# A two-layer hybrid block: the first two output slabs worked by halves, and three steps moved between engines

## What is computed

```python
def mixer_ab(u, pos, w_in, w_out, ...):
    z = u @ w_in
    za, zb = z[..., :A_IN], z[..., A_IN:]
    ...
    ya = diff_attention(qa, ka, va, lam, subln_g, lambda_init)
    yb = rwkv7_time_mix(zb, mu, w0, w2, a0, a2, g2, k_k, k_a, r_k, lnx_g, lnx_b)
    return jnp.concatenate([ya.astype(u.dtype), yb.astype(u.dtype)], axis=-1) @ w_out
```

```python
    y = wkv7_scan(heads(r), heads(decay), heads(k), heads(v), -kk, kk * heads(a).astype(jnp.float32))
    mu_y = jnp.mean(y, axis=-1, keepdims=True)
    var_y = jnp.mean(jnp.square(y - mu_y), axis=-1, keepdims=True)
    y = (y - mu_y) * lax.rsqrt(var_y + LNX_EPS)
    y = y * lnx_g... + lnx_b...
    bonus = jnp.sum(heads(r) * heads(k) * r_k, axis=-1, keepdims=True) * heads(v)
    y = (y + bonus.astype(jnp.float32)).reshape(B, T, B_WIDTH) * g.astype(jnp.float32)
```

## Time and profile before

| what | value |
|---|---|
| median of three runs | 2696.46 us (2686.87 to 2701.3) |
| the profiled execution, its own time | 2687.12 us |
| its span, first to last instruction | 2685.4 us |
| TensorE busy | 2525.0 us, 94% of the span |
| VectorE, ScalarE, GpSimd busy | 1443.8, 1082.8 and 266.1 us |
| mean granted TensorE clock | 0.976 of full speed |

### The profile page before, as it was taken

One profiled execution on the slowest core, in us unless ns is written; L12 is line 12 of the kernel. 1 busy time (PEld: TensorE's weight loads), 2 busy tenths in 40 slices (PEclk: granted clock), 3 DMA queues, 4 the chain that ended last, 5 costly groups with the idle time before them and its releaser, 6 DMA issues.

```text
span 2685.4 us, 33969 instructions
## 1 busy us (share of the span) xinstructions
PE 2525.0 (94%) x14359; PEld 2083.3 (78%) x14359; DVE 1443.8 (54%) x1447; ACT 1082.8 (40%) x1167; POOL 266.1 (10%) x239
## 2 busy tenths in 40 slices
PE   8999987889999999999988998898999999999897
PEld 6887767678888878878766977786888888888775
DVE  4566774645544445445454567646544545445454
ACT  4455420344434334334434444545434334334432
POOL 3001343111000000000122000012000000000121
PEclk9999999999999999999998999998999999999998
DMA  7556401356555555555543654255555565555542
GB/s 260 187 176 206 137 26 68 133 180 207 184 192 188 188 175 186 190 178 181 188 142 103 192 176 152 75 192 192 188 188 189 187 195 187 188 196 179 181 144 75
DMA packets 224819, 453.22 MB, mean 169 GB/s; under 512 B 7833, under 2 KB 16343, under 8 KB 223403
## 3 DMA queue, kind: packets, MB, share of 16 engines
q1 hardware_dynamic: 218816, 430.11, 48.5%
q0 software_dynamic: 3648, 17.54, 1.9%
q10 hardware_dynamic: 2219, 3.59, 0.5%
HBM read 445.52 MB, written 2.10 MB: 167 GB/s over the span
## 4 chain that ended last, share of the span: by engine, by line
PE 85%; DVE 8%; ACT 3%; issue 2%; ACTq 1%; DMA 0%; SPq 0%; DVEq 0%
PE psum L294 26%; PE psum L296 26%; PE psum L295 26%; DVE wlo L276 2%; ACT whi L272 2%; DVE h L441 1%; PE psum L596 1%; PE psum L712 1%; PE psum L318 1%; PE psum L1444 1%; PE psum L1440 1%; PE psum L1425 0%; ACT junk L386 0%; ACTq L992 0%; DVE m L686 0%
## 5 line engine op out<-in xcount | busy, mean ns | idle before, releaser
L276 DVE TENSOR_TENSOR wlo<-raw,whi 128x2048 fp32r<-128x2048 f32 (+1 forms) x404 | 929.9, 2302 | 1057.0 <-ACT whi L272 1056.8
L272 ACT ACTIVATE whi<-raw 128x2048 fp32r<-128x2048 f32 (+1 forms) x408 | 775.0, 1900 | 1232.9 <-PE psum L296 1226.5
L294 PE MATMUL psum<-whi,uTh 128*128 128x512 f32 (+2 forms) x2240 | 882.7, 394 | 18.0 <-DVE uTl L340 10.7
L296 PE MATMUL psum<-whi,uTl 128*128 128x512 f32 (+2 forms) x2240 | 871.1, 389 | 6.3 <-issue 6.3
L295 PE MATMUL psum<-wlo,uTh 128*128 128x512 f32 (+2 forms) x2240 | 870.5, 389 | 0.0
L294 PEld LDWEIGHTS psum<-whi,uTh 128*128 128x128 f32 x2240 | 424.4, 189 | 111.2 <-issue 11.9
L296 PEld LDWEIGHTS psum<-whi,uTl 128*128 128x128 f32 x2240 | 423.7, 189 | 92.1 <-issue 7.2
L295 PEld LDWEIGHTS psum<-wlo,uTh 128*128 128x128 f32 x2240 | 424.2, 189 | 82.7 <-issue 1.7
L294 PE MATMUL psum<-whi,hTh 128*128 128x512 f32 x1024 | 400.6, 391 | 6.1 <-DVE wlo L276 6.1
L296 PE MATMUL psum<-whi,hTl 128*128 128x512 f32 x1024 | 398.6, 389 | 0.0
L295 PE MATMUL psum<-wlo,hTh 128*128 128x512 f32 x1024 | 398.5, 389 | 0.0
(11 more groups left out here) (348 smaller groups left out, 1493.8 us busy)
## 6 DMA issues: line engine op xcount, KB each, us to landing
raw<-in_w_mlp_up SPq DMA_DIRECT2D x128, 1024.0 KB, 5.2
raw<-in_w_mlp_down SPq DMA_DIRECT2D x128, 1024.0 KB, 5.1
raw<-in_ab_w_in SPq DMA_DIRECT2D x48, 1024.0 KB, 5.1
raw<-in_w_ple_gate SPq DMA_DIRECT2D x32, 1024.0 KB, 5.1
raw<-in_c_w_in SPq DMA_DIRECT2D x24, 1024.0 KB, 5.3
raw<-in_ab_w_out SPq DMA_DIRECT2D x16, 1024.0 KB, 5.3
raw<-in_c_w_out SPq DMA_DIRECT2D x16, 1024.0 KB, 5.0
raw<-in_c_w_in SPq DMA_DIRECT2D x12, 736.0 KB, 4.4
```

Source lines behind the costliest of these rows:

```text
L272: act.activation(whi[:, q % 2, :, 0:n], raw[:, q, :, 0:n], ACT.Copy).then_inc(hi_ready, 1)
L276: dve.tensor_tensor(wlo[:, q % 2, :, 0:n], raw[:, q, :, 0:n], whi[:, q % 2, :, 0:n].bitcast(F32), ALU.subtract).then_inc(lo_ready, 1)
L294: pe.matmul(o, xh, hi, start=(q == 0 and k == 0), stop=False)
L296: last = pe.matmul(o, xl, hi, start=False, stop=(q == 3 and k == 3))
```

## The change

Five things change, all within layer 0's mixer.

1. **Attention norm first.** `subln_dve` is cut in two. Its sum over squares (`subln_sum_dve`) moves ahead of `level_d_dve(0, 3)`, and its chain of tiny instructions (`subln_rms_dve`) goes to the place of the bonus sum. The bonus sum goes to the place of the old norm.
2. **Squares on ScalarE.** The squares of `out_norm_dve` part 2 become one ScalarE instruction for each token tile (`y_square_act`), between VectorE's centring and its sum.
3. **All lows on VectorE.** GpSimd no longer makes the lows of chunks 2 and 3 of the first output slab. VectorE's lows of chunks 0 and 1 are made earlier.
4. **Slabs in pairs.** The first two slabs of `ab_out` are worked as eight chunks: attention rows of slab 0, attention rows of slab 1, recurrence rows of slab 0, recurrence rows of slab 1. Loads, splits, matmuls and read-outs follow this order, and part 4 of `out_norm_dve` is cut into two parts (4 and 5), one for each half of the columns.
5. **Semaphores.** Two parameter loads now share one semaphore, and one step of `tt_init_pool` shares that of its setup.

```diff
-        dve.wait_ge(sem("bonus"), 2)
-        dve.tensor_reduce(bon[:], heads4(rkr[:]), AX.X, ALU.add).then_inc(sem("bon"), 1)
+        subln_rms_dve(dve, link)
         level_y_dve(dve, 0, 4)
         level_d_dve(dve, 1, 1)
         level_d_dve(dve, 0, 4)
-        subln_dve(dve, link)
+        dve.wait_ge(sem("bonus"), 2)
+        dve.tensor_reduce(bon[:], heads4(rkr[:]), AX.X, ALU.add).then_inc(sem("bon"), 1)
...
         u_out_dve(dve, 2)
+        split_lo(dve, base["ab_out"], 0)
         st_dve(dve, 2)
-        for k in range(4):
-            out_norm_dve(dve, link, 0, k)
-        prologue(split_lo, dve, "ab_out")
-        out_norm_dve(dve, link, 0, 4)
+        out_norm_dve(dve, link, 0, 0)
+        out_norm_dve(dve, link, 0, 1)
+        split_lo(dve, base["ab_out"], 1)
+        out_norm_dve(dve, link, 0, 2)
+        out_norm_dve(dve, link, 0, 3)
...
-        split_hi(act, base["ab_out"], 0)
+        prologue(split_hi, act, "ab_out")
         x_out_act(act, 3)
+        y_square_act(act, 0)
         u_out_act(act, 3)
-        split_hi(act, base["ab_out"], 1)
         y_out_act(act, 1)
+
+    def y_square_act(act, tt):
+        act.wait_ge(sem("y_centred"), tt + 1)
+        act.activation((sq0, Xs)[tt][:], rv[:, tt, :], ACT.Square).then_inc(sem("y_sq"), 1)
...
-        pool.wait_ge(lo_ready, 4 * base["ab_out"] + 2)
-        for q in (2, 3):
-            split_lo(pool, base["ab_out"], q)
...
+    OUT_CHUNKS = (((0, 0), (0, 1), (1, 0), (1, 1)), ((0, 2), (0, 3), (1, 2), (1, 3)))
...
+    def out_pair_pe(pe, st, src, ready):
+
+        T_pe(pe, st, src, ready, 0)
+        for v in range(2):
+            for q in range(4):
+                j, kc = OUT_CHUNKS[v][q]
+                s = base[st] + j
+                if v == 0 and q == 0:
+                    T_pe(pe, st, src, ready, 1)
+                if v == 0 and q == 2:
+
+                    pe.wait_ge(sem("y_out"), 2)
+                if v == 0 and q == 3:
+                    T_pe(pe, st, src, ready, 2)
+                    T_pe(pe, st, src, ready, 3)
+                pe.wait_ge(*mark("xT_lo", st, 2 * kc + 2))
+                pe.wait_ge(lo_ready, 4 * (base[st] + v) + q + 1)
...
-        pool.dma_start(p_ka[:], A["rwkv_k_a"][0].partition_broadcast(P)).then_inc(sem("ka_in"), 16)
+        pool.dma_start(p_ka[:], A["rwkv_k_a"][0].partition_broadcast(P)).then_inc(sem("ka_rk_in"), 16)
```

More of the change, by code:

```diff
@@ L747, in ple_dve, with out_keep_act @@
             step(split_lo, dve, s, st, W if j < 3 else next_width(st), gated, skip=(j == 0), last=(j == 3))
+    OUT_CHUNKS = (((0, 0), (0, 1), (1, 0), (1, 1)), ((0, 2), (0, 3), (1, 2), (1, 3)))
+    def out_keep_act(act, st, j, done):
+        s = base[st] + j
+        act.wait_ge(mm_used, done)
+        if j == 0:
+            act.wait_ge(*mark("xT", st, 8))
+        for tt in range(TT):
+            square(act, bank[2 * (s % 2) + tt][:], ssq[:, tt, j:j + 1], *mark("m_sq", st, 2 * j + tt + 1))
+        for tt in range(TT):
+            last = act.activation(m[:, tt, j * W:(j + 1) * W], bank[2 * (s % 2) + tt][:], ACT.Copy)
+        last.then_inc(sem("m_out"), 1)
@@ L750, in out_act @@
     def out_act(act, st):
+        s = base[st]
         if st == "ab_out":
             act.wait_ge(sem("y_mm"), 2)
[L754 to L768, removed]
@@ L770, in out_dve @@
-    def out_dve(dve, link, st):
[L771 to L778, removed]
-        if st == "ab_out":
-            dve.wait_ge(lo_ready, 4 * base[st] + 4)
-        for j in range(4):
-            step(split_lo, dve, base[st] + j, st, W if j < 3 else next_width(st), None, skip=(j == 0), last=(j == 3))
+            T_act(act, st, 0)
@@ new lines, in out_pair_pe @@
+    def out_pair_pe(pe, st, src, ready):
+        T_pe(pe, st, src, ready, 0)
+        for v in range(2):
+            for q in range(4):
+                j, kc = OUT_CHUNKS[v][q]
+                s = base[st] + j
+                if v == 0 and q == 0:
[7 more added lines that the diff above has]
+                pe.wait_ge(lo_ready, 4 * (base[st] + v) + q + 1)
+                for k in range(4):
+                    for tt in range(TT):
+                        o = bank[2 * (s % 2) + tt][:]
+                        xh = uTh[:, 4 * kc + k, tt * P:(tt + 1) * P]
+                        xl = uTl[:, 4 * kc + k, tt * P:(tt + 1) * P]
+                        hi, lo = whi[:, q % 2, k, :], wlo[:, q % 2, k, :]
+                        pe.matmul(o, xh, hi, start=(kc == 0 and k == 0), stop=False)
+                        pe.matmul(o, xh, lo, start=False, stop=False)
+                        last = pe.matmul(o, xl, hi, start=False, stop=(kc == 3 and k == 3))
+                last.then_inc(mm_used, 1)
@@ L785, in out_pe @@
     def out_pe(pe, st, src, ready):
-        for j in range(4):
-            if st == "ab_out" and j == 1:
-                pe.wait_ge(sem("y_out"), 2)
+        if st == "ab_out":
+            out_pair_pe(pe, st, src, ready)
+        for j in range(2 if st == "ab_out" else 0, 4):
             s = base[st] + j
```

92 lines of the change are left out of this document (71 added, 21 removed).

## The result

| what | before | after |
|---|---|---|
| median of six runs | 2693.86 us (2686.87 to 2702.59) | 2676.86 us (2671.26 to 2678.17) |
| profiled execution, and its span | 2687.12, 2685.4 | 2678.17, 2676.4 |
| mean granted TensorE clock | 0.976 | 0.975 |

The ratio is 0.9928, with a 95% interval of 0.9912 to 0.9943: 0.7% faster, 17.0 us by the medians. The forecast was 2677.9 us, a gain of 18.6. The profiled executions lie only 9.0 us apart. That of before lies at the low end of its runs, and that of after was the slowest of its six.

What follows compares the result with a forecast made beforehand. TensorE, busy 94% of the span, was taken as the bound, so only its waits could give time back. 11.7 + 8.1 - 1.2 = 18.6 us off the 2696.5 us median gave 2677.9 us, range 2664 to 2691.

Steps and rivals of the forecast that it cites:

- Term 1: Layer 0's mixer: with the attention norm moved, TensorE's wait for Y goes and the next link runs faster; 11.7 us gained.
- Term 2: End of the recurrence and first output chunks: TensorE starts earlier and the stage ends at 586.5 instead of 594.6; 8.1 us.
- Term 3: New TensorE pauses ahead of chunk 0 and chunk 2: lower clock after the latter loses 1.2 us, bounds 0 and 2.4.
- Copies beside GpSimd at 0: VectorE's PSUM copies of Xs and Us beside GpSimd's steps are not held: cost 0, bounded by 9.5 us.
- No slack for the squares: ScalarE's first squares end at 486.1, its last Us started at 486.09: each microsecond VectorE is late costs one.
- Only the norm pays: Rival, chance 0.15: VectorE bounds the first output chunks, whose gain falls to about 2 us; time 2684.
- Copies are held: Rival, chance 0.07: VectorE's copies of Xs and Us are held beside GpSimd, costing 9.5 us; time 2687.4.
- GpSimd holds the chain: Rival, chance 0.04: after the bonus sum GpSimd's steps hold thirteen VectorE chain instructions, costing 30.8 us; time 2708.7.
- the change does not do what it says: Rival, chance 0.04: the norm's tiny instructions stay slow in their new place, some 12 us; 2690 results.
- the sum is made on the profile and shifted to the median: Whole kernel: the 18.6 us worked out on the 2687.1 us profiled execution was subtracted unchanged from the 2696.5 us median.
- the sign that the prediction named against its chain as the path: Layer 0's mixer: if TensorE's 10.3 us pause goes but time falls under 10 us, the chain-is-the-path argument is wrong.

Runs made afterwards that it cites:

- x_late_again: Changed kernel with the reload of x issued behind the third slab's loads, measured once more as a base: 2669.21 us, ratio 0.9912.
- changed_again: The changed kernel itself, unaltered, measured once more: 2675.16 us, ratio 0.9942 to the kernel before.
- squares_dve: As x_late, with the squares of the output norm back on VectorE: 2667.8 us, ratio 0.9907.
- x_late: Changed kernel with the reload of x issued behind the third slab's loads instead of behind the first four chunks: 2668.3 us, ratio 0.9923.
- norm_undone: Changed kernel with the attention norm put back behind the bonus sum, all else as changed: 2681.65 us, ratio 0.9968.
- pool_quiet: Kernel before, with GpSimd waiting for the end of the attention norm before its eight bonus steps: 2685.67 us, ratio 0.9992.
- norm_only: Kernel before with only the attention norm moved ahead of the bonus sum: 2683.97 us, ratio 0.9976.
- x_shifted: Changed kernel with the reload of x held until the last state update is done: 2666.52 us, ratio 0.9918.
- lows_pool: As x_late, with the lows of the third and fourth chunk back on GpSimd: 2672.4 us, ratio 0.9924.

## Why the prediction was right, point by point

- **Term 1, 11.7 us.** Right in the trace. From the start of the chain's 128 matmuls to that of the next link it is 10.24 us less (forecast 10.25), and the link takes 2.08 us instead of 3.50, 1.42 less (forecast 1.45). The sum over squares in its new place cost nothing. SP's first load went out at 439.95 (forecast 438.7), and nobody waited for it. In the times of whole runs the norm's move brought 6.5 us, see below.
- **Term 2, 8.1 us.** Its mechanism was right and its size near, 8.75 us in x_late_again. From `Xs` to the first matmul the forecast had 22.06 us and the run 20.09; of the 1.97 less, 1.47 is the pause that the forecast had copied from before. From the first matmul to the third chunk it had 13.6, the run 13.79. The rest of the stage was 78.4 against 78.1. In the profile of after the term does not appear, see above.
- **Term 3, minus 1.2 us.** Half right, and small. In the changed kernel the third chunk starts behind a pause of 2.38 us, and the clock is 0.54 there. In changed_again, the same kernel, it stays at 1.00 behind 2.36 us. In x_late_again the pause is 1.02 and the clock stays at 1.00. The loss behind its first pause vanished in this later wait, as forecast, which is why the wait is 1.02 and not the 2.6 us of the sum.
- **Copies beside GpSimd at 0.** Right: 0.68 us for `Xs` and `Us` at 430.48 and 435.13, with GpSimd at work from 421.53 to 448.4. The rules of the Trainium skill (page "SBUF — State Buffer", section "Who interferes with whom"; page "VectorE: DVE Perf Modes", section "Why PSUM operands drop a tier") held on both sides here. The tiny instructions that read SBUF were held, up to 4.49 us, and the reads of PSUM were not.
- **No slack for the squares.** The first squares end at 481.57 + 1.06 = 482.63, and the next `Us` starts at 482.93 after a wait of 0.30 us for TensorE. So they cost nothing. By the trace of squares_dve they bring about 1 us, which its runs don't show.
- **The rivals.** "Only the norm pays": refuted, the rest alone gives 0.9968. "Copies are held", "GpSimd holds the chain" and "the change does not do what it says": refuted by the rows above.

**What was missing from the sum** is the reload of `x`. I had no term for it, though the pause of 1.47 us stands in the timeline of before. Against x_late it costs the changed kernel 6.9 us. The profiled pair differs by 9.0 us, 9.6 less than the 18.6 of the sum: 0.9 are missing at `Xs`, 6.5 from there to the next stage, and 2.2 go behind the mixer.

That the median still came out within about 1 us of the forecast rests on a second omission on the other side. I took all terms from a profiled execution at the low end of the runs and carried them to the median unchanged. But the profiled pair differs by 9.0 us and the medians by 17.0. So typical runs of before lose some 7 us that its profile does not show, and where they lose them is not known. The last microsecond or two come from the median of before, which fell from 2696.46 to 2693.86 us with three more runs. The errors nearly cancel; the agreement is partly luck. The step that failed is "the sum is made on the profile and shifted to the median", and beside it the missing row for the reload.

**Why step 1 brings 6.5 us and not 11.7** stays open. With the norm in its old place the reload's pause is 1.47 us (before), 1.96 (norm_undone) and 1.81 (pool_quiet), each with a clock of 1.00 behind it. With the norm moved it is 2.91, 4.00 (changed kernel, twice) and 3.18 (norm_only), each with a fall of the clock. A different phase of the reload against the recurrence is not the reason: in all six profiles it is issued 4.64 us ahead of ScalarE's `Xs` (467.80 and 472.44 before, 457.03 and 461.67 after). What has come closer is the first slab's loads, 17.1 us ahead of the reload instead of 37.3. But in pool_quiet they are as close (440.05 and 457.19), and the pause is 1.81. In norm_only TensorE's pause of 10.3 us is gone and the time has fallen by less than 10 us. That is the sign that the prediction named against its chain as the path; here the reload's pause (3.18 us instead of 1.47) and the low clock (485.21 - 467.60 = 17.61 us to the last group of L1533 instead of 12.98) took 6.3 us of what the chain gave. A test of the grouping would be x_late with the norm undone, which was not run.

## What to carry to other kernels

When an engine's wait is removed, look through the traces of before for small pauses marked "issue" that remain. Here one of 1.47 us became 2.91 to 4.00 us with a fall of the clock behind it, though the reload beside it was issued at the same point of the chain. Try to put bulk loads that nobody needs soon outside stretches of many tiny matmuls: it brought 6.9 us in the changed kernel and nothing in the old one. And before adding a sum worked out on one profiled run to a median, ask what the other runs lose that this one doesn't.

## What was not expected of the hardware

**Instruction loads share the DMA engines.** The trace has a DMA queue of kind "instruction". In the recurrence of x_late_again it moves packets of 16 KB at 454.6, 458.6 and 462.0 us, so 4.0 and 3.4 us apart. In the changed kernel, where the reload is under way, the DMA view of the half microsecond from 462.5 has one again:

```profile
q1 hardware_dynamic: 86, 0.18, 94.0%
q8 instruction: 1, 0.02, 11.0%
```

The packet ahead of it was at 456.0, so 6.8 us lie between them. Put together from narrow windows of this kind (0.2 us each):

| kernel | packet before | next packet | between | TensorE's pause | goes on at |
|---|---|---|---|---|---|
| x_late_again | 454.6 | 458.6 | 4.0 | none | |
| before | 466.4 | 472.2 | 5.8 | 1.47 | 474.73 |
| pool_quiet | 456.2 | 462.0 | 5.8 | 1.81 | 464.46 |
| norm_undone | 468.6 | 475.2 | 6.6 | 1.96 | 477.79 |
| after | 456.0 | 462.8 | 6.8 | 2.91 | 465.40 |
| norm_only | 458.0 | 465.0 | 7.0 | 3.18 | 467.60 |
| changed_again | 454.0 | 461.8 | 7.8 | 4.00 | 464.37 |
| x_shifted | 466.6 | 473.2 | 6.6 | none | |

In the six profiles with a pause, the longer the gap, the longer the pause (two gaps of 5.8 apart), and TensorE goes on 2.5 to 2.6 us after the packet. This fits a TensorE that has run out of instructions whose load is held up by the reload. In x_shifted the gap is as long and there is no pause; there it falls at the end of the recurrence. The reading is inferred from times, and no run changed the instruction load alone.

The gap alone is no measure of a delay: with the DMA engines nearly idle it is 5.0 us in before (461.4 to 466.4) and 5.6 in x_late_again (462.0 to 467.6), and TensorE does not pause. Pauses of the same kind also stand under or just behind the first slab's loads, and the late reload doesn't take them away: 1.77 us at 445.11 in before, 1.30 and 1.05 at 448.57 and 453.64 in x_late_again.

The Trainium skill, page "DMA: Bandwidth & Descriptors", section "Queues, rings and completion order", says that a DMA engine turns from one queue to the next after each packet. By that an instruction packet would wait for about one packet of the reload. That is an estimated 0.1 us if it is a packet as the trace counts them (1088 packets of 2 KB in the 15 us from 455, at a share of 42% of 16 engines). The section gives 9 to 17 descriptors to a packet; if each of the trace's packets is one descriptor, the estimate is 0.8 to 1.6 us. The gaps in the rows with a pause are 1.8 to 3.8 us longer than the 4.0 of x_late_again at that place, so at least the longer ones need something else besides.

**How long the lower clock lasts differs, and the pause ahead of it doesn't tell.** Behind the 2.52-us pause in x_late_again the full-size matmuls run at the 1.2 GHz level from about 481.7 to 485 and then at 2.4 GHz again. Behind the 2.91-us pause of the changed kernel the small 64x64 matmuls stay at the lower level from about 466 to 480, though TensorE is busy throughout by the windows above. It is not the small matmuls alone: in lows_pool, behind a pause of 2.15 us in the recurrence, they are back at the upper level after 3 us:

```profile
453.45:456.50 3.05, 3.05 (x61) 3.05 (x62) 0.75 (x1) 0.00 (x0) 0.00 (x0) 0.54 0.02 5
456.50:480.00 23.50, 21.85 (x605) 20.58 (x601) 14.20 (x25) 11.16 (x15) 0.00 (x0) 1.00 0.29 93
```

Nor does the length of one pause decide whether the clock falls. In x_shifted it is low behind 1.28 us, in changed_again it is not behind 2.36 us:

```profile
448.00:452.50 4.50, 4.26 (x95) 4.26 (x97) 0.69 (x1) 0.00 (x0) 0.00 (x0) 0.62 0.66 241
```
```profile
502.00:506.00 4.00, 3.43 (x15) 2.89 (x16) 3.86 (x7) 0.21 (x1) 0.00 (x0) 1.00 0.57 190
```

What decides it is shown by no run here.
